# Joining the input load with the first norm, and the embedding gates with the row turns and norms around them, in a one-core two-block model kernel

## What is computed

```python
def rmsnorm(x, g):
    xf = x.astype(jnp.float32)
    y = xf * lax.rsqrt(jnp.mean(xf * xf, axis=-1, keepdims=True) + EPS)
    return (y * g.astype(jnp.float32)).astype(x.dtype)

def first_block(x, p, ...):
    h = x
    for i in range(DEPTH):                      # DEPTH = 2
        hn = rmsnorm(h, norm_g[i])
        m = even_layer(hn, ...) if i % 2 == 0 else odd_layer(hn, ...)
        h = h + m
        h = h + jax.nn.sigmoid(h @ ple_w_gate[i]) * (p[i] @ ple_w_proj[i])
    return h
```

## Time and profile before

| | us |
|---|---|
| median of 3 runs | 2969.78 |
| lowest and highest of them | 2965.21, 2978.34 |
| profiled execution | 2970.92 |
| its span, first to last instruction | 2969.1 |

### The profile page before, as it was taken

One profiled execution on the slowest core, in us unless ns is written; L12 is line 12 of the kernel. 1 busy time (PEld: TensorE's weight loads), 2 busy tenths in 40 slices (PEclk: granted clock), 3 DMA queues, 4 the chain that ended last, 5 costly groups with the idle time before them and its releaser, 6 DMA issues. The chain is left out here.

```text
span 2969.1 us, 37794 instructions
## 1 busy us (share of the span) xinstructions
PE 2640.1 (89%) x15472; PEld 1434.4 (48%) x15472; DVE 781.6 (26%) x1719; ACT 536.3 (18%) x1269; POOL 488.4 (16%) x710
## 2 busy tenths in 40 slices
PE   6997898989868999999699999959999879999994
PEld 3654445445564445466455555524445444544441
DVE  2305211333331032151411111120346341211112
ACT  2105101322230021250100001011244210100000
POOL 1526101034210122170000000020234100000001
PEclk9997898997969999998799999979999789999997
DMA  4221003101001041011699999963010059999996
GB/s 168 65 77 43 29 32 105 49 10 71 31 3 37 13 153 67 27 47 55 233 409 411 411 411 411 411 245 117 2 58 30 29 229 385 411 411 411 411 411 246
DMA packets 180226, 532.34 MB, mean 179 GB/s; under 512 B 21312, under 2 KB 31424, under 8 KB 180096
## 3 DMA queue, kind: packets, MB, share of 16 engines
q1 hardware_dynamic: 167488, 505.22, 44.0%
q10 hardware_dynamic: 10240, 16.79, 1.6%
q0 software_dynamic: 2368, 8.52, 0.8%
HBM read 507.26 MB, written 23.10 MB: 179 GB/s over the span
## 5 line engine op out<-in xcount | busy, mean ns | idle before, releaser
L374 PE MATMUL psum<-weight_ring,hidden_T 128*128 128x512 f32 (+3 forms) x1664 | 658.3, 553 | 15.1 <-DMA arena<-in_p_T 11.4
L374 PEld LDWEIGHTS psum<-weight_ring,hidden_T 128*128 128x128 f32 x1664 | 314.9, 195 | 333.7 <-issue 258.5
L2694 PE MATMUL psum<-hidden_T,arena 128*128 128x128 f32 x2304 | 287.9, 281 | 21.5 <-DVE hidden_T L2689 21.5
L2694 PEld LDWEIGHTS psum<-hidden_T,arena 128*128 128x128 f32 x2304 | 271.0, 194 | 70.7 <-issue 48.7
L2705 PE MATMUL psum<-arena,hidden_T 128*64 128x512 f32 x1344 | 295.8, 592 | 0.0
L2717 PE MATMUL psum<-weight_ring,hidden_T 128*64 128x512 f32 x1024 | 239.4, 610 | 39.1 <-DMA weight_ring<-in_moe_w_down 38.2
L2941 POOL DMA_INDIRECT arena<-expert_rows_out,arena x18 | 20.9, 1158 | 1087.3 <-issue 548.6
L2705 PEld LDWEIGHTS psum<-arena,hidden_T 128*64 128x64 f32 x1344 | 100.5, 137 | 188.1 <-issue 188.1
L2705 PE MATMUL psum<-weight_ring,hidden_T 128*64 128x512 f32 x704 | 155.0, 592 | 0.0
L2717 PEld LDWEIGHTS psum<-weight_ring,hidden_T 128*64 128x64 f32 x1024 | 72.1, 139 | 159.7 <-issue 138.5
L374 PE MATMUL psum<-weight_ring,arena 128*128 128x512 f32 (+2 forms) x320 | 122.6, 525 | 11.8 <-PEq L1017 10.8
(11 more groups left out here) (508 smaller groups left out, 2878.5 us busy)
## 6 DMA issues: line engine op xcount, KB each, us to landing
arena<-in_moe_w_up SPq DMA_DIRECT2D x84, 2048.0 KB, 24.0
weight_ring<-in_moe_w_down SPq DMA_DIRECT2D x64, 2048.0 KB, 24.0
weight_ring<-in_moe_w_up SPq DMA_DIRECT2D x44, 2048.0 KB, 23.4
expert_rows_out<-arena ACTq DMA_DIRECT2D x128, 128.0 KB, 5.6
weight_ring<-in_hg_w_in SPq DMA_DIRECT2D x8, 2048.0 KB, 10.6
weight_ring<-in_ev_w_in SPq DMA_DIRECT2D x8, 1536.0 KB, 6.8
weight_ring<-in_fox_w_in SPq DMA_DIRECT2D x6, 2048.0 KB, 8.1
weight_ring<-in_od_w_in SPq DMA_DIRECT2D x5, 2048.0 KB, 7.9
```

Of the source, the lines that this page charges most:

```text
L374: last = nc.tensor.matmul(out, l, r, start=i == 0, stop=i == len(left) - 1)
L2694: last = nc.tensor.matmul(g.psum[:, c // 4, (c % 4) * P:(c % 4 + 1) * P], keep[:, i, c * P:(c + 1) * P], row[:, i, :], start=i == 0, stop= ...
```

## The change

`stage_load` and the first `stage_norm` become one stage, `stage_load_norm`. x is loaded in four pieces, one for each row tile, each with a semaphore of its own. The vector engine waits for positions and constants only, works the angles of the sine, squares tile 2, works the angles of the cosine, squares tile 4, and then moves the turned tiles. The scalar engine squares tiles 1 and 3, scales all four into buffers of their own, and does sine and cosine last. Gains are waited for ahead of the moves, and the meta tokens by the load queue alone.

`stage_ple` takes in the row turns ahead of it and the norm behind it. Its units are ordered by tile now, both halves of a tile in a row, and a list (`turns`, `behind`) says which turns stand on TensorE behind which tile's units: the raw turns two tiles ahead of their use, the norm of tile t - 1 behind the units of tile t. Turns use the four upper PSUM banks. For the second layer the norm covers the meta tile as well. `stage_norm` is gone, also from `odd_layer` and `fox_layer`. Each gate stage feeds the ring as far as the norm stage behind it did. The names of the semaphores of the experts' pieces are shared with the new ones.

```diff
-def stage_load(g):
+def stage_load_norm(g, gain, ring_upto):
...
         @block.sync
         def _(sp):
-            sp.dma_start(pos_i, ...).then_inc(*loaded.up(16))
-            sp.dma_start(g.const[:, :], ...).then_inc(*loaded.up(16))
-            sp.dma_start(g.h[:, 1:5, :], a["x"].rearrange("b (t p) d -> p (b t) d", p=P)).then_inc(*loaded.up(16))
-            sp.dma_start(g.gains[:, :], a["norm_gains"]).then_inc(*loaded.up(16))
+            sp.dma_start(pos_i, ...).then_inc(*tables.up(16))
+            sp.dma_start(g.const[:, :], ...).then_inc(*tables.up(16))
+            for i in range(4):
+                sp.dma_start(g.h[:, 1 + i, :], x[:, i, :]).then_inc(*row_in[i].up(16))
+            sp.dma_start(g.gains[:, :], a["norm_gains"]).then_inc(*gains_in.up(16))
             sp.wait_ge(*zeroed.at(1))
-            sp.dma_start(g.h[0:META, 0, :], a["meta_tokens_2"]).then_inc(*loaded.up(16))
-            g.feed(sp, 3)
-            sp.wait_ge(*loaded.at(80))
+            sp.dma_start(g.h[0:META, 0, :], a["meta_tokens_2"]).then_inc(*meta_in.up(16))
+            g.feed(sp, ring_upto)
+            sp.wait_ge(*meta_in.at(16))
...
         @block.vector
         def _(dve):
-            dve.wait_ge(*loaded.at(80))
+            dve.wait_ge(*tables.at(32))
...
+                i = 2 * n + 1
+                dve.wait_ge(*row_in[i].at(16))
...
+                nc.vector.tensor_tensor_reduce(out=sq[:, 1, :], in0=g.h[:, 1 + i, :], in1=g.h[:, 1 + i, :], ...).then_inc(*squared_v.up())
+            dve.wait_ge(*gains_in.at(16))
+            for i, t in enumerate(XT):
...
         @block.scalar
         def _(act):
+            for i in (0, 2):
+                act.wait_ge(*row_in[i].at(16))
+                if i:
+                    act.wait_ge(*squared.last())
+                nc.scalar.activation(sq[:, 0, :], g.h[:, 1 + i, :], ACT.Square, accum_out=ss[:, i:i + 1]).then_inc(*squared.up())
+            for i in range(4):
+                act.wait_ge(*rooted.at(i + 1))
+                nc.scalar.activation(rows[:, i, :], g.h[:, 1 + i, :], ACT.Copy, scale=rs[:, i:i + 1]).then_inc(*scaled.up())
             for n, dst in enumerate((g.sin, g.cos)):
...
+        @block.tensor
+        def _(pe):
+            for i in range(4):
+                pe.wait_ge(*scaled.at(i + 1))
+                if i >= 2:
+                    pe.wait_ge(*moved.at(2 * (i - 1)))
...
-def stage_norm(g, tiles, gain, ring_upto, keep=None, ahead=None):
...
-def stage_ple(g, layer, chunks, proj_chunk, ring_upto):
+def stage_ple(g, layer, chunks, proj_chunk, tiles, gain, ring_upto):
...
+    few = [0] if 0 in tiles else []
+    order = few + list(XT)
+    nth = {t: i for i, t in enumerate(order)}
+    turns = [("raw", 1), ("raw", 2)]
+    behind = {1: [("raw", 3)] + [("norm", t) for t in few], 2: [("raw", 4), ("norm", 1)], 3: [("norm", 2)], 4: [("norm", 3), ("norm", 4)]}
+    for t in XT:
+        turns += behind[t]
+    at = {job: j for j, job in enumerate(turns)}
+    slot = lambda j: 4 + 2 * (j % 2)
     with nc.Block() as block:
         @block.tensor
         def _(pe):
+            def turn(job):
+                j, (kind, t) = at[job], job
+                n = TILES[t][1]
+                if kind == "norm":
+                    pe.wait_ge(*scaled.at(nth[t] + 1))
+                if j >= 2:
+                    pe.wait_ge(*moved.at(2 * (j - 1)))
+                for c in range(KD):
+                    src = rows[0:n, nth[t] % 2, ...] if kind == "norm" else g.h[0:n, t, ...]
+                    last = nc.tensor.transpose(g.psum[:, slot(j) + c // 4, ...], src, ...)
+                last.then_inc(*transposed.up())
+
+            turn(("raw", 1))
+            turn(("raw", 2))
             u = 0
-            pe.wait_ge(*p_in.at(16))
-            g.weights_wait(pe, proj_chunk)
-            for half, chunk in enumerate(chunks):
-                g.weights_wait(pe, chunk)
-                for t in XT:
-                    a, n = TILES[t]
-                    if u - 1 > 0:
+            for t in XT:
+                a, n = TILES[t]
+                pe.wait_ge(*moved.at(2 * (at["raw", t] + 1)))
+                for half, chunk in enumerate(chunks):
+                    if t == 1:
+                        g.weights_wait(pe, chunk)
+                    if u >= 2:
                         pe.wait_ge(*gated.at(u - 1))
                     rows_by_weights(g, pe, g.psum[:, u % 2, :], t, chunk).then_inc(*ready.up())
+                    if u == 0:
+                        g.weights_wait(pe, proj_chunk)
+                        pe.wait_ge(*p_in.at(16))
...
+                for job in behind[t]:
+                    turn(job)
...
         @block.scalar
         def _(act):
...
+            for t in few:
+                square(t)
+                scale(t)
+            for t in XT:
+                sigmoid(2 * t - 2)
+                if t > 1:
+                    square(t - 1)
+                sigmoid(2 * t - 1)
+                if t > 1:
+                    scale(t - 1)
+            square(4)
+            scale(4)
...
         @block.vector
         def _(dve):
...
+            move(("raw", 1))
+            move(("raw", 2))
+            for t in XT:
+                multiply(2 * t - 2)
+                multiply(2 * t - 1)
+                for job in behind[t]:
+                    move(job)
...
         @block.gpsimd
         def _(pool):
...
+            for t in few:
+                root(t)
+            for t in XT:
+                add(2 * t - 2)
+                if t > 1:
+                    root(t - 1)
+                add(2 * t - 1)
+            root(4)
...
-        stage_load(g)
         even, even_out = plans["even"]
-        stage_norm(g, XT, g.gain(0), even[3])
+        stage_load_norm(g, g.gain(0), even[3])
...
-        stage_norm(g, XT, None, g.fed)
-        stage_ple(g, 0, gate, proj, gate[1] + 4)
+        stage_ple(g, 0, gate, proj, XT, g.gain(1), plans["odd"][0][0] + 4)
...
-        stage_norm(g, XT, None, g.fed)
-        stage_ple(g, 1, gate, proj, gate[1] + 4)
+        stage_ple(g, 1, gate, proj, ALLT, g.gain(2), plans["fox"][0] + 4)
```

165 lines of the change are left out of this document (74 added, 91 removed).

## The result

| | runs | median us | lowest, highest |
|---|---|---|---|
| before | 4 | 2967.59 | 2965.21, 2978.34 |
| changed | 4 | 2933.78 | 2930.22, 2939.39 |

The ratio is 0.9881, with a 95% interval of 0.9862 to 0.9900: 35 us less, between 30 and 41. The forecast was 2942 us, 28.9 us under its base, with a range from 2933 to 2952. The direction and the mechanism held; the gain came out larger by 5 to 6 us. The median lies 0.8 us inside the low end of the range, and 0.9881 times the median before, 2932.3 us, lies 0.7 us outside it. Two more measurements of the same kernel, further down, gave 0.9873 and 0.9902 (0.9888 to 0.9917, so 25 to 33 us, which holds the forecast 28.9). Over all 13 executions of it and 36 of the kernel before, the medians are 2935.3 and 2968.6, 33.3 us apart.

What follows compares the result with a forecast made beforehand. TensorE was taken as the bound at three places, idle while small steps run on other engines. Gains of 9.5 (start), 7.9 (layer 0 gates) and 11.5 (layer 1 gates) sum to 28.9 us: 2970.9 to 2942 us, range 2933 to 2952.

Steps and rivals of the forecast that it cites:

- the tail of both gate stages: End of each gate stage: 6.35 us to the last turn, 2.0 cold turn, 1.8 to next product, 10.15 us in all.
- the clock charge behind the tails: Stages after the gates start at a slow TensorE clock: 2.7 us in layer 0, 1.0 in layer 1, each between 0 and 3.0.
- Start: Load joined with first norm: first product at 20.7 us instead of 30.22, gain 9.5 us, bounds nothing and 12.7.
- the 8.05 us behind it: At the start, first transposition to first product, taken as unchanged at 8.05 us.
- rival 1: At the start, the four loads of x do not stream; start gains 0 to 1.5 us, time 2951 us, chance 0.10.
- Gates, up to the last product: Both gate stages: first product 2.4 us in, 8 units at 8.58 us (68.7), turns between units 3.9 us in layer 0.
- the turn of norm 2: TensorE turn of tile 2's norm between gate units; waits 0.35 us for its scale.
- Rival 2: Joined streams stall each other in the gates; both stages together lose 10 us, time 2952 us, chance 0.10.
- The last turn of layer 1: End of layer 1's gates: one cold turn of 2.0 us.
- a best end of 2937: Whole kernel: all clock costs at zero and the start a little better give 2937 us.
- Rivals 3 and 4: 3: slow TensorE clock through both gate stages, 3080 us, chance 0.02; 4: something later sets the pace, 2970 us, 0.04.
- the signs of being wrong: Inner norm turns waiting over 1 us each, first weights after 20 us, or a stage behind 1060 us taking longer.

Runs made afterwards that it cites:

- the one-load kernel: Changed kernel with x in one load again, all tiles behind one semaphore; first product at 23.75 us instead of 20.39.
- two kernels with the same gates: Changed kernel with x in one load, and with tile 1's scale ahead of tile 3's square at the start; odd mixer's first stage 146.2 us in both.
- The run with the idle square: Changed kernel plus one idle vector-engine instruction per gate tail, a square in layer 0, a copy in layer 1; layer 0 product to last turn 8.35 us instead of 7.33.

## Where the prediction held, and which terms it mis-sized

The mechanism held, and the sum did not. The step that failed first is the tail of both gate stages: 6.35 us from the last product to the last turn, because the chain through GpSimd's root was taken as unchanged. The runs show 5.45 us in both layers. The second is the clock charge behind the tails, a single 2.7 us for the odd mixer; its first stage lost 4.7 us in two profiles of the changed kernel and nothing in the third.

Between 2942 and 2933.8 lie 8.2 us. 3.3 are the base (2970.9 against the median of 2967.6). 4.9 are the gain, 33.8 instead of 28.9: the three places gave 36.3 instead of 32.6, and 2.5 of it is missing from the difference of the medians, instead of the 3.7 charged for the clock. That 2.5 is a difference between one pair of profiles and the medians, and not measured anywhere.

**Start.** Right. Predicted 9.5 us, measured 9.8 at the place and 9.6 at the end when done alone. What the forecast lacks is the even mixer behind it: 1.7 us less in its first stage, with the clock at 1.00 at its start instead of 0.57 (in the kernel with only the start joined it began at 0.57 again, and took 200.8). Tile 3's load decided the first turn (12.53 against 12.6 predicted), the 8.05 us behind it were 7.86. The loads streamed, so rival 1 fell; the one-load kernel puts a number on it.

**Gates, up to the last product.** Right. Products began 2.45 us in, in both layers, eight units kept 8.58 us, the load of p was hidden, the turn of norm 2 waited 0.17 us (0.35 predicted). From the first product to the end of the last, 72.7 us were measured in layer 0 and 73.5 in layer 1, against 72.9 and 73.9. Rival 2 found no place: no inner turn stalled, and GpSimd's add beside a move of the vector engine took 1.26 us (at 449.65, the move at 449.93) as it had alone, so taking 0 for that was right.

**The tail: mis-sized.** I took 6.35 us from the last product to the last turn, out of the separate norm of before, and said that "the chain through multiply, add, square, root and scale is the same for tile 4, less one boundary". It is 5.45 (448.79 to 454.24). Of the 1.2 us to the old 6.65, 0.3 are the boundary, as predicted. The rest is the root: before, the vector engine squared tile 4 at that moment, and its square stretched the power on GpSimd from 0.55 to 1.46 us; joined, all squares are on the scalar engine and the root runs alone. The run with a square put back shows it: 6.47 us. I had weighed this contention in one direction only, as a cost that the change might add, and had priced a root at its contended time. That is 0.9 us in each layer.

**The last turn of layer 1** took 1.32 us at a clock of 0.77, not 2.0: 0.7 us. From the last turn to the next product it was 1.65 us in both layers, not 1.8.

**The clock behind the tails: mis-sized in both directions.** I charged 2.7 us to the odd mixer and 1.0 to the forget stage. The first began slow as predicted, and by the count of records (10 and 9 instead of 16) its first 6 us lost 2.2 to 2.6 us, near the 2.7 charged. But I took the start's loss for the stage's. Over the whole stage three profiles gave 151.0, 151.0 and 146.15 us, and two kernels with the same gates 146.2, against 146.3 before: 4.7 or nothing. The run with the idle square had 148.6, the kernel with only the gates joined 151.2. What I had missed is that the stage as it was before loses too, though it began at 1.00: with idle matmuls ahead, in the changed kernel, it takes 143.9. The forget stage lost 0.3 to 0.6 of the 1.0 charged; its clock was 0.62 in its first 6 us, and had been below full speed before too, 0.72.

**The sum.** Local gains without clock charges: predicted 9.5 + 10.6 + 12.5 = 32.6, measured 36.3. Of the 3.7 between them, 1.8 are the root, 0.7 the warm turn, 0.3 the start, 0.7 the stretch of products and turns, the rest boundaries. With the charges I forecast 28.9; the profiled pair gave 31.5, with the odd mixer at 151.0; the pooled medians say 33.3. The three measurements say 33.8, 36.7 and 29.6, so how far the forecast is off at the end is known to a few us only; the terms at the places are known to a tenth.

**The base and the range.** I built on the profiled execution at 2970.9; the median of before is 2968.6 over 36 executions, and they reach from 2957.5 to 2978.3. The changed kernel's 13 reach from 2927.5 to 2943.0. This scatter goes with TensorE's mean granted clock: 2927.5 us at 0.938 and 2943.0 at 0.932, some 2.3 us for each 0.001 over the 13. I had given it 4 us below a best end of 2937. From the base 2970.9 a real gain of 33 to 34 is that best end itself, and it took nearly the whole allowance for scatter to hold the median. That 2933.8 lies inside the range by 0.8 us is luck. The Trainium skill (TensorE: Matmul & The Clock Gate, part 1) says that the number of slow matmuls differs between runs of one kernel, and I had cited it for one term of 2.7 us. The trace agrees, but for more stages than that one. In the three profiles of the changed kernel the even mixer's second stage took 93.8 to 95.4 us, the odd mixer's first 146.2 to 151.0, and the latent attention, which nothing here edits, 54.5 at a clock of 0.90 and 59.4 at 0.79.

**Rivals 3 and 4.** TensorE's clock stayed at full speed between the units, and the stages at a flat 411 GB/s came earlier as a block: the third fell, and the fourth too. One of the signs of being wrong did show: from 1213.55 us on, behind the forget stage, 763.8 us passed to the next stage boundary listed for TensorE, 1.4 more than before. It proves nothing either way, as this stretch took 761.5 to 766.7 us over all the profiles. And 84.2 and 84.3 us lie under the 85 to 88 that the forecast gave for the gates, by the tails.

What stays open: what decides between the 151 us and the 146, how much of the joined norms' and the idle matmuls' gain reaches the end, and so the gain of the whole to better than some 4 us.

## What to carry to other kernels

When small stages that wait for each other are merged, add up the chain anew with the instructions that will stand beside it, and not only the ones in it: a step on GpSimd may have been priced while the vector engine held it. Here the turns and norms that hid between products cost their TensorE time and at most 0.17 us of waiting, each with at least part of a unit of products to get ready. And a term for TensorE's clock after a rest is a spread and not a number: the stage behind it lost 0 or 4.7 us in profiles of one kernel, so it belongs in the range's width, at both ends. What is gained at a place is measured there to a tenth of a us; what of it reaches the end of a kernel whose executions lie 15 us apart needs many more executions than four.

## What the runs showed of the hardware

GpSimd's scale-and-add on 128 x 1 elements was held to the end of the vector engine's instruction beside it: 0.19 us alone, 0.69 beside a 128 x 1024 copy, 1.22 beside a 128 x 1024 square. Its power took 0.55 alone and 1.46 and 1.64 beside a square, and ended 0.4 us after it. Its 128 x 512 add took 1.26 both alone and beside the vector engine's move out of PSUM. The Trainium skill (GPSIMD Engine Reference, key points) names contention with vector instructions that have two SBUF inputs or run in a two-port mode. The traces agree for the square, which has two inputs; the copy has one, and no trace here shows in which mode it ran.

Four loads of 512 KB on one queue landed 1.28 us apart (from tiles 1 and 3, 2.55 us), at the rate of one load of 2048 KB, 5.1 us behind the constants before. The Trainium skill (DMA: Bandwidth & Descriptors, rules for kernel authors) wants at least 1 MiB in a DMA for the most bandwidth. No loss of that kind shows here; splitting gained 3.4 us.

Ten matmul records of pure filler, 4.46 us, kept the clock at 1.00 through a rest of 4.35 us that otherwise brought it to 0.50 in layer 0 and 0.77 in layer 1. The stage behind it in layer 0 took 143.9 us in all four profiles with them, and 145.6 to 151.2 in the ten without, before included. The kernel's median moved by less than its scatter.
